# Order of the high and low matmuls within a half unit: from pairs to eight high, then eight low

## What is computed

```python
for i in range(DEPTH):                       # DEPTH = 2
    h = rmsnorm(x, norm_mix_g[i])
    if i % 2 == 0:
        x = x + even_mixer(h, w_in_even[j], w_fnet[j], w_out_even[j], rel_bias_table)
    else:
        x = x + diff_attention(h, w_qkv_odd[j], w_out_odd[j], ...)
    x = x + sqrelu_mlp(rmsnorm(x, norm_ffn_g[i]), w_ff1[i], w_ff2[i])   # 2048 -> 8192 -> 2048
return rmsnorm(x, norm_final_g)
```

## Time and profile before

| | |
|---|---|
| median of 3 timed runs | 2213.97 us (2213.47 to 2214.65) |
| the profiled execution | 2215.82 us, its span 2214.0 us |
| TensorE busy with matmuls | 2181.9 us (99%), 12644 matmuls |
| VectorE busy | 1529.4 us (69%) |
| ScalarE busy | 1034.5 us (47%) |
| from HBM | 402.7 MB, 183 GB/s over the span |

### The profile page before, as it was taken

The page is one execution under the profiler, slowest core; times in us unless marked ns, Lnnn a source line. Parts: engine busy times, 40 slices in busy tenths (PEclk is TensorE's granted clock), DMA queues, the critical chain, the costliest instruction groups (busy, mean ns, idle before and its releaser), DMA issues.

```text
span 2214.0 us, 36865 instructions
## 1 busy us (share of the span) xinstructions
PE 2181.9 (99%) x12644; PEld 1908.1 (86%) x12644; DVE 1529.4 (69%) x2299; ACT 1034.5 (47%) x1465; POOL 29.1 (1%) x32
## 2 busy tenths in 40 slices
PE   6999999999999999999999999999999999999997
PEld 5888888888888888888888888888888888888886
DVE  7777767765765675677777777777656656756765
ACT  4444445543443443455554454555434434534553
POOL 3000000000000000000000000000000000000000
PEclk9999999999999999999999999999999999999998
DMA  8444446555555555555544444455555555555552
GB/s 286 170 163 164 169 170 207 194 191 190 187 190 189 189 189 189 187 188 192 176 170 172 171 169 157 180 180 188 190 189 190 190 189 189 186 191 183 186 191 87
DMA packets 64439, 405.65 MB, mean 183 GB/s; under 512 B 6615, under 2 KB 15831, under 8 KB 16380
## 3 DMA queue, kind: packets, MB, share of 16 engines
q1 hardware_dynamic: 61838, 401.71, 50.7%
q10 hardware_dynamic: 2174, 2.17, 0.3%
q0 software_dynamic: 368, 0.99, 0.1%
HBM read 402.70 MB, written 2.14 MB: 183 GB/s over the span
## 4 chain that ended last, share of the span: by engine, by line
issue 78%; PE 20%; DVE 1%; DMA 0%; ACT 0%; POOL 0%; DVEq 0%; SPq 0%; POOLq 0%; ACTq 0%
PE acc L954 12%; PE acc L957 6%; DMA x<-xT_dram 0%; PE ps_scores L996 0%; PE ps_o L996 0%; PE ps_aux L1064 0%; DVE gx L604 0%; PE ps_attn_t L1028 0%; ACT gx L336 0%; DVE w_lo L543 0%; PE ps_scores L1051 0%; DVE bias L210 0%; POOL rstd_col L283 0%; PE ps_v L1017 0%; DVEq L81 0%
## 5 line engine op out<-in xcount | busy, mean ns | idle before, releaser
L543 DVE TENSOR_TENSOR w_lo<-raw,w_hi 128x1024 fp32r<-128x1024 f32 x752 | 918.0, 1225 | 321.0 <-ACT w_hi L310 306.5
L954 PE MATMUL acc<-gx,w_hi 128*128 128x512 f32 x3440 | 1089.1, 398 | 9.6 <-DVE gx L604 9.1
L310 ACT ACTIVATE w_hi<-raw 128x1024 fp32r<-128x1024 f32 x752 | 795.8, 1058 | 617.1 <-PE acc L957 613.8
L954 PE MATMUL acc<-mid,w_hi 128*128 128x512 f32 x2560 | 805.1, 396 | 0.3 <-DVE mid L894 0.3
L957 PEld LDWEIGHTS acc<-gx,w_lo 128*128 128x128 f32 x3440 | 648.3, 188 | 153.1
L957 PE MATMUL acc<-gx,w_lo 128*128 128x256 f32 x3440 | 678.1, 279 | 0.0
L957 PEld LDWEIGHTS acc<-mid,w_lo 128*128 128x128 f32 x2560 | 480.9, 188 | 113.6
L954 PEld LDWEIGHTS acc<-gx,w_hi 128*128 128x128 f32 x3440 | 526.4, 189 | 13.6 <-DVE gx L604 8.9
L957 PE MATMUL acc<-mid,w_lo 128*128 128x256 f32 x2560 | 502.9, 278 | 0.0
L954 PEld LDWEIGHTS acc<-mid,w_hi 128*128 128x128 f32 x2560 | 390.1, 189 | 0.8 <-DVE mid L894 0.7
L317 ACT ACTIVATE copied<-acc 128x256 f32<-128x256 f32 x215 | 82.3, 383 | 353.6 <-PE acc L957 349.3
(11 more groups left out here) (100 smaller groups left out, 520.1 us busy)
## 6 DMA issues: line engine op xcount, KB each, us to landing
raw<-weights_dram SPq DMA_DIRECT2D x375, 1024.0 KB, 4.8
x<-xT_dram SPq DMA_DIRECT2D x4, 512.0 KB, 9.2
bias<-bias_line SPq DMA_DIRECT2D x2, 1024.0 KB, 7.2
bias<-bias_line ACTq DMA_DIRECT2D x2, 1024.0 KB, 9.6
raw<-weights_dram SPq DMA_DIRECT2D x2, 512.0 KB, 6.2
bias<-bias_line SPq DMA_DIRECT2D x2, 512.0 KB, 6.4
out_dram<-bias SPq DMA_DIRECT2D x2, 512.0 KB, 3.8
out_dram<-bias SPq DMA_DIRECT2D x2, 384.0 KB, 3.2
```

What stands on the lines that cost most here:

```text
L310: act.activation(w_hi[:, n % RING, :], raw[:, u % RAW_SLOTS, part * HALF:(part + 1) * HALF], ACT.Copy).then_inc(hi_ready, 1)
L543: dve.tensor_tensor(w_lo[:, n % RING, :], raw[:, u % RAW_SLOTS, part * HALF:(part + 1) * HALF], w_hi[:, n % RING, :].bitcast(F32), ALU.sub ...
L954: pe.matmul(acc_of(u)[:], w_hi[:, n % RING, cols], operand[:, kt, :], start=kt == 0, stop=False)
```

## The change

In half, the eight high matmuls are issued first and then the eight low ones. The wait for lo_ready moves between the two, and at the head stands a wait for hi_ready in its place. The hooks and tile waits stay with the high matmuls, so they stand ahead of all low ones; w_used still rises with the last matmul of the half. The number of matmuls, their operands and all other engines' code are the same.

```diff
@@ -942,7 +942,7 @@
             def half(n, u, kts, operand, o=0, hooks=None, whole=None, tile_wait=None):
 
                 hooks = hooks or {}
-                pe.wait_ge(lo_ready, n + 1 + 2 * o)
+                pe.wait_ge(hi_ready, n + 1 + 2 * o)
                 for j, kt in enumerate(kts):
                     for step in hooks.get(j, ()):
                         step()
@@ -950,12 +950,12 @@
                         ready, base, first = tile_wait
                         if kt == 0 or kt >= first:
                             pe.wait_ge(ready, base + (kt + 1 if kt else first))
-                    cols = slice(j * P, (j + 1) * P)
-                    pe.matmul(acc_of(u)[:], w_hi[:, n % RING, cols], operand[:, kt, :], start=kt == 0, stop=False)
-                    if j % 2:
-                        for i in (j - 1, j):
-                            ins = pe.matmul(acc_of(u)[:, SEQ:], w_lo[:, n % RING, i * P:(i + 1) * P],
-                                            operand[:, kts[i], 0:SEQ], start=False, stop=kts[i] == KT - 1)
+                    pe.matmul(acc_of(u)[:], w_hi[:, n % RING, j * P:(j + 1) * P], operand[:, kt, :], start=kt == 0,
+                              stop=False)
+                pe.wait_ge(lo_ready, n + 1 + 2 * o)
+                for j, kt in enumerate(kts):
+                    ins = pe.matmul(acc_of(u)[:, SEQ:], w_lo[:, n % RING, j * P:(j + 1) * P], operand[:, kt, 0:SEQ],
+                                    start=False, stop=kt == KT - 1)
                 ins.then_inc(w_used, 1)
                 for step in hooks.get(KT // 2, ()):
                     step()
```

## The result

The changed kernel takes 2221.34 us (median of 7 runs, 2220.64 to 2222.1) against 2214.64 for the kernel before beside it: ratio 1.003, interval 1.0021 to 1.004. It is 0.3% slower. Its profiled execution has a span of 2220.1 us, 6.1 more than before.

The account below looks back on a forecast made before the run. TensorE's matmul stream was taken as the bound; 0 + 0 + 0 + 0.7 + 0.7 - 0.2 = +1.2 us gave 2217.0 us profiled, 2215.2 us on the timed scale, with a range of 2192 to 2236 us.

Parts of the forecast that it names:

- no change but the small terms: Likeliest case for the whole kernel: only the small start, output projection and hook terms count, 2213 to 2218 us; chance 0.42.
- the slower rival: In each half's long low run, low matmuls cost more from the third on: 2229 to 2244 us; chance 0.25.
- Slower than +0.2%: Whole-kernel outcome: measurably slower, from dearer long low runs or from the added wait or slipped hooks; chance 0.33.
- What bounds the kernel: Whole kernel: TensorE's own matmul stream, busy 99% of 2214.0 us; a high and low pair takes 348.1 ns.
- Part 1: Head of each half: waiting for hi_ready in place of lo_ready releases nothing sooner; gain 0.
- Part 2: Ahead of each half's first low matmul: 752 more waits on TensorE, already satisfied, cost 0.
- The rival that gave it 10 ns: Ahead of each half's first low matmul: the added wait costs 10 ns each, +7.5 us, 2223 us; chance 0.08 including slipped hooks.
- Part 3: Matmul order within each half: eight high then eight low leaves the half at 2785 ns; 0.
- Part 5: Hooks within halves come sooner: stat_spread gains 0.2 us; turn_attn in layer 1 just holds, taken as 0.
- Part 4: Late operand tiles: six low matmuls no longer fill the gap, +0.7 us at the start, +0.7 in the last output projection.
- L in a long run is dearer: Low runs in each half: 118.3 to 122 ns per low matmul, high staying at 233; 2229 to 2244 us; chance 0.25.
- The cost sits at the change of kind: Within each half: each high/low change costs 4.9 ns, so fewer changes save 22 us, 2193 us; chance 0.20.

Follow-up runs that it names:

- e2: The kernel before, order kept (two high, two low, four times), with the change's waits, lo_ready ahead of the first low matmul: 2215.05 us, ratio 0.9999.
- e1: The change's order, but lo_ready waited for at the head of the half, so without the added wait: 2219.69 us, ratio 1.0024 against the kernel before.
- e5: The change with low matmuls of 128 columns in place of 256, part of the computation left out: 2186.24 us.
- e6: The change with low matmuls of 128 columns, seven of eight loading only 64 weight columns, more computation left out: 1952.31 us.
- e9: The change with low matmuls of 256 columns, seven of eight loading 64 weight columns in place of 128, part of the computation left out: 2195.35 us.
- e7: The change with lo_ready at the head and low matmuls first in SECOND halves without hooks or tile waits (runs of sixteen): 2215.03 us, ratio 0.9999.
- e8: As e7, but the order of the kernel before in every half with a hook or tile wait: 2212.40 us, ratio 0.999 against the kernel before.
- e3: The kernel before with high and low matmuls alternating one by one, lo_ready at the head: 2239.37 us, ratio 1.0084.

## Why the prediction was right or wrong

The time came out inside the range of 2192 to 2236 us, but in neither of its two likeliest places: 2221.34 is above the 2213 to 2218 of "no change but the small terms" and below the 2229 to 2244 of the slower rival. "Slower than +0.2%", which it is, had a chance of 0.33. The span lost 6.1 us where 1.2 were forecast. By its steps:

- **What bounds the kernel** held: TensorE's stream, with no wait for weights before or after.
- **Part 1, hi_ready in place of lo_ready: 0.** Right. e2 has the two waits with the old order and is at 0.9999.
- **Part 2, the added wait: 0.** Right by the same run, and by e1, which has the order without it and the same 2793.3 ns. The rival that gave it 10 ns, 7.5 us in all, is refuted: e2's interval ends at +0.08%, 1.8 us.
- **Part 3, the order: 0.** This is the term that was mis-sized: it measured +6.6 ns a half in the MLPs, +4.9 us in all but the start and the last output projection (3.0 + 1.9 in the table; the hooks of Part 5 add some tenths, the 26 halves behind scores take as much off). The reason given for taking 0, that a dearer L may be paid for by a cheaper H, was half of the truth: in the run the sum does fall, 120.0 + 226.7 = 346.7 ns against 348.3. What was missed is that the high run begins with five matmuls that are not yet cheap. The L are 31 ns a half dearer than in pairs, the H 24 cheaper. Over 752 halves either alone would be 23 or 18 us (an estimate), so that the time stayed near the forecast is in part luck: the prediction named a cheaper H as possible, but had no row that said how much. Its 348.1 ns for a pair is 348.3 by single stamps; nothing hangs on that.
- **Part 4, late tiles: +0.7 and +0.7.** Right, the one at the start with luck. The starts of the kernel after at the beginning:

```profile
23.66 1.22 PE L953 MATMUL acc<-gx,w_hi 128*128 128x512 f32 x2 [1.70 <-DVE gx L604]
24.68 1.91 PE L957 MATMUL acc<-gx,w_lo 128*128 128x256 f32 x8
26.38 3.44 PE L953 MATMUL acc<-gx,w_hi 128*128 128x512 f32 x8
29.66 1.11 PE L957 MATMUL acc<-gx,w_lo 128*128 128x256 f32 x8
30.61 1.09 PE L953 MATMUL acc<-gx,w_hi 128*128 128x512 f32 x4
```

  Half 0 ends 26.38 - 25.05 = 1.33 us later, and the unit 30.61 - 29.91 = 0.70 us, since its low matmuls now run at the full level. That is the 0.70 foretold, on the condition that the low level ends at the same time again, which it did here. In e1, with the same order, it ended 2 us earlier, and the same unit ended at 29.51 us, 0.4 before that of the kernel before. In the last output projection:

```profile
1398.47 1.70 PE L996 MATMUL ps_o<-v_tok,attn_t 128*128 128x256 f32 x12 [0.49 <-DVE v_tok L581]
...
1405.08 0.89 PE L953 MATMUL acc<-mid,w_hi 128*128 128x512 f32 x2 [0.75 <-DVE mid L894]
...
1406.77 1.55 PE L953 MATMUL acc<-mid,w_hi 128*128 128x512 f32 x6
```

  The wait for v_tok is 0.49 us (0.46 foretold), and from the H behind the wait for mid to the next half it is now 1.69 us where it was 0.97: +0.72.
- **Part 5, hooks.** stat_spread: TensorE waits 0.35 us where it waited 0.57, -0.2 as foretold. turn_attn had 0.05 us to spare, and that did not quite hold:

```profile
1163.41 0.88 DVE L872 SCALAR_TENSOR_TENSOR attn<-logits,lam_inv,pos_dft 128x256 f32<-128x256 f32 x2
...
1164.42 0.65 PE L1028 MATMUL ps_attn_t<-ident,attn 128*128 128x128 f32 x4
```

  VectorE ends at 1164.29 and the transposes start at 1164.42; in six of the eight heads the gap ahead of them is 267 or 340 ns where 230 is usual, 0.4 us together. It lies within the 0 to 0.8 us that were given.

Of the rivals, "L in a long run is dearer" was right in its price per L, 120.0 against its 118.3 to 122, and as far as e5, e6 and e9 tell in its mechanism, the load (e9 against e1: 113.3 against 120.0). It was wrong in "the H stay at 233". "The cost sits at the change of kind" gave 225 for an H in a run, and 226.7 was measured, but the alternating order, with the most changes, also has a stretch that loses nothing against the settled gaps, 2773 ns a half. Each had one half of the gaps right, and they nearly cancel. What decides the remainder, the gaps behind a change, neither had.

**What stays open** is what the disturbance is. It follows the same numbers (233, 236, 228, 233, 231) in the change, e1, e7, e8 and e9 in nearly every high run that stands directly behind eight or sixteen L. It is not the wait, not a difference between eight and sixteen L, not the place in the half and not the loads of those L. Six L996 matmuls between shorten it to two H. With pairs a half comes out cheaper than with fours, and H L H L runs for long stretches without loss or with some 50 ns a half of it. Calling this a state is an argument from these numbers; no run here tells what it is.

## What to carry to other kernels

On a TensorE that waits for nothing, the order of wide and narrow matmuls still moves the time by some tenths of a per cent to one per cent (2212 to 2239 us here, with the same matmuls), and not monotonically with the length of the runs: measure the gap from start to start over a period of the order, don't add up gaps taken from another order. Moving a semaphore wait buys nothing unless a row shows someone waiting at it; work that used to fill the gap ahead of a late operand and is moved behind it, on the other hand, costs its own time, here 0.7 us at each of two places (at the start only with the clock's rise at the same moment).

## What the runs showed of the hardware

- A low matmul of 128 columns with a load of 128 weight columns comes every 112 ns, with 64 weight columns every 60 (e5, e6): there the load, not the columns, sets the pace. At 256 columns and a full load the gap is 120 (the change, e1), above both the 112 of e5 and the 107 of the columns.
- The same instruction pattern ran at 347 and at 353 ns a pair in different stretches of one execution (e3), at the same granted clock; whole executions differed by 15 us.
- The same half of eight H and eight L took 2793 ns behind another such half and 2776 ns behind six matmuls by L996 (all 26 such halves of the change and of e1).
- At the low level of the clock no such overhead is seen: L start 213 ns apart and H 427 at the program's start, which is 256 and 512 columns at 1.2 GHz. The level is read from the starts; the window rows print a granted clock of 1.00 there too.
